# Modulation sums along weight rows on DVE, the first shift vector on TensorE, and layer 0's first input tiles completed pair by pair

## The reference

```python
c_act = jax.nn.silu(c)                                   # c is (1, 1024)
for l in range(2):
    mod = (c_act @ ada_w[l] + ada_b[l])[:, None, :]      # ada_w[l] is (1024, 6 * 1024) f32
    sh_m, sc_m, g_m, sh_f, sc_f, g_f = jnp.split(mod, 6, axis=-1)
    h = rms_norm(x, norm_mix_pre[l]) * (1 + sc_m) + sh_m
    x = x + g_m * rms_norm(hybrid_mixer(h, ...), norm_mix_post[l])
    h = rms_norm(x, norm_ffn_pre[l]) * (1 + sc_f) + sh_f
    x = x + g_f * rms_norm(ffn(h), norm_ffn_post[l])
```

## Time and profile before

| | |
|---|---|
| three runs | 1609.78, 1613.15, 1611.60 us; median 1611.6 us |
| profiled execution | 1613.58 us, of it the span of instructions 1611.8 us |
| busy share of the span | PE 95%, PEld 82%, DVE 84%, ACT 62%, POOL 4% |
| mean granted TensorE clock | 0.983 of full |
| DMA | 507.48 MB, mean 315 GB/s |
| PE busy and DMA share in slices of 40 us, first five | PE 3, 9, 9, 9, 9 tenths; DMA 9, 9, 5, 7, 6 tenths |

### The profile page before, as it was taken

One profiled execution on the slowest core, in us unless ns is written; L12 is line 12 of the kernel. 1 busy time (PEld: TensorE's weight loads), 2 busy tenths in 40 slices (PEclk: granted clock), 3 DMA queues, 4 the chain that ended last, 5 costly groups with the idle time before them and its releaser, 6 DMA issues.

```text
span 1611.8 us, 21543 instructions
## 1 busy us (share of the span) xinstructions
PE 1537.8 (95%) x8256; PEld 1328.5 (82%) x8256; DVE 1352.7 (84%) x1245; ACT 1007.1 (62%) x861; POOL 70.7 (4%) x99
## 2 busy tenths in 40 slices
PE   3999989999899998999999999999999999999995
PEld 3899979999789977888888887888887888888884
DVE  6987787775778867899899898899898899998885
ACT  3573443433456344777777777777777777777773
POOL 6000000000000000000000000000000000000000
PEclk9999999999999998999999999999999999999998
DMA  9957657775574862999999999999999999999990
GB/s 375 365 182 259 244 229 288 287 254 191 180 251 173 303 221 105 360 384 358 404 374 358 395 381 361 375 380 366 395 375 352 384 376 368 392 376 365 410 368 28
DMA packets 72705, 507.48 MB, mean 315 GB/s; under 512 B 8096, under 2 KB 8224, under 8 KB 13856
## 3 DMA queue, kind: packets, MB, share of 16 engines
q1 hardware_dynamic: 68528, 491.40, 79.8%
q0 software_dynamic: 4080, 14.69, 3.1%
HBM read 499.24 MB, written 6.82 MB: 314 GB/s over the span
## 4 chain that ended last, share of the span: by engine, by line
PE 89%; DVE 6%; ACT 2%; issue 1%; POOL 1%; DMA 0%; DVEq 0%; ACTq 0%; POOLq 0%
PE ps L1348 28%; PE ps L1350 27%; PE ps L1349 27%; PE ps L1744 1%; DVE lo L849 1%; DVE r L901 1%; PE ps L1387 1%; DVE lo L880 1%; DVE ada_acc L813 1%; PE ps L1511 1%; PE ps L1494 1%; PE ps L1367 1%; DVE x_tok L936 1%; DMA router_bias<-in_router_bias_dram 0%; ACT hi L515 0%
## 5 line engine op out<-in xcount | busy, mean ns | idle before, releaser
L880 DVE TENSOR_TENSOR lo<-raw,hi 128x2048 fp32r<-128x2048 f32 x336 | 764.8, 2290 | 96.9 <-ACT hi L515 96.4
L515 ACT ACTIVATE hi<-raw 128x2048 fp32r<-128x2048 f32 x336 | 644.8, 1919 | 200.4 <-PE ps L1350 200.4
L1348 PE MATMUL ps<-hi,hT_hi 128*128 128x512 f32 (+2 forms) x1088 | 428.9, 394 | 11.8 <-DVE hT_lo L907 4.8
L1350 PE MATMUL ps<-hi,hT_lo 128*128 128x512 f32 (+2 forms) x1088 | 420.8, 387 | 0.0
L1349 PE MATMUL ps<-lo,hT_hi 128*128 128x512 f32 (+2 forms) x1088 | 420.2, 386 | 0.0
L1348 PEld LDWEIGHTS ps<-hi,hT_hi 128*128 128x128 f32 x1088 | 205.2, 189 | 56.5 <-issue 8.4
L849 DVE TENSOR_TENSOR lo<-raw,hi 128x2048 fp32r<-128x2048 f32 (+2 forms) x87 | 190.1, 2190 | 62.0 <-ACT hi L499 60.6
L1350 PEld LDWEIGHTS ps<-hi,hT_lo 128*128 128x128 f32 x1088 | 205.1, 188 | 41.1
L1349 PEld LDWEIGHTS ps<-lo,hT_hi 128*128 128x128 f32 x1088 | 205.5, 189 | 38.2 <-issue 0.5
L1348 PE MATMUL ps<-hi,bT_hi 128*128 128x512 f32 (+1 forms) x576 | 226.7, 394 | 1.8 <-DVE bT_lo L1259 1.8
L499 ACT ACTIVATE hi<-raw 128x2048 fp32r<-128x2048 f32 (+2 forms) x87 | 158.3, 1824 | 108.5 <-PE ps L1350 105.4
(11 more groups left out here) (259 smaller groups left out, 1227.5 us busy)
## 6 DMA issues: line engine op xcount, KB each, us to landing
raw<-in_moe_w_dram SPq DMA_DIRECT2D x336, 1024.0 KB, 7.1
raw<-in_w_ada_dram SPq DMA_DIRECT2D x48, 1024.0 KB, 5.2
raw<-in_w_fg_dram SPq DMA_DIRECT2D x11, 1024.0 KB, 5.3
raw<-in_w_fu_dram SPq DMA_DIRECT2D x11, 1024.0 KB, 5.1
raw<-in_w_fd_dram SPq DMA_DIRECT2D x11, 1024.0 KB, 5.7
raw<-in_w_ga_dram SPq DMA_DIRECT2D x8, 1024.0 KB, 6.8
raw<-in_w_gb_dram SPq DMA_DIRECT2D x8, 1024.0 KB, 5.5
raw<-in_w_ab_dram SPq DMA_DIRECT2D x8, 1024.0 KB, 4.9
```

The costliest lines, as they stand in the source:

```text
L515: act.activation(hi[:, s, :], raw[:, slot, :], ACT.Copy).then_inc(hi_done, 1)
L880: dve.tensor_tensor(lo[:, s, :], raw[:, slot, :], hi[:, s, :].bitcast(f32), ALU.subtract).then_inc(raw_done, 1)
L1348: pe.matmul(o, wh, mh, start=first, stop=False)
L1350: return pe.matmul(o, wl, mh, start=False, stop=last)
```

## The change

Four things are changed together.

1. **Modulation weights by output channel.** The weights are laid out so that a partition holds one output channel's 1024 weights; a quarter holds two such blocks of 128 channels. `silu(c)` is repeated on all partitions (`cbc`, a broadcast DMA of 0.5 MB and one ACT pass), and DVE multiplies and sums along the row in one instruction (`scalar_tensor_tensor` with `accum_out`), which gives one finished column of the vector `av`. The sums over partitions on PE, and their uses on DVE, go away for shift and scale vectors. Gates build their diagonal in one DVE pass (`ada_gate`) and keep their two matmuls.
2. **The first shift vector on PE.** Its weights keep input channels on partitions (`w_ada0`); `shift_sum` makes 16 matmuls with one moving column per quarter, straight from `raw`; DVE adds the bias (`ada_shift`).
3. **The start pair by pair.** The stream brings shift and scale quarters alternately, x after the first of them, and the two cq chunks between them. Each quarter pair completes two channel blocks of scale and shift, and DVE, ACT and PE take up the layer input block pair by block pair. ACT's sine of the rotary angles moves behind the cq chunks.
4. **Layer 0's feed-forward shift vector** moves from chunks 2 to 5 to chunks 8 to 11 in `ADA_AT`.

```diff
-ADA_AT = [(0, SH_F, M0 + 2), (0, SC_F, M0 + 13), (0, G_M, M0 + 18),
+ADA_AT = [(0, SH_F, M0 + 8), (0, SC_F, M0 + 13), (0, G_M, M0 + 18),
...
-    out = [("ada", a, q) for a in range(len(ADA_FIRST)) for q in range(4)]
-    for s in range(NW):
+    out = []
+    for q in range(4):
+        if q >= 2:
+            out.append(("w", q - 2, 0))
+        out += [("ada", 0, q), ("ada", 1, q)]
+    for s in range(FIRST_W, NW):
...
+            sp.dma_start(cbc[:, :], A["c"].to_broadcast([P, D])).then_inc(cbc_in, 16)
...
-                if r == NRAW - 2:
+                if r == 0:
                     sp.dma_start(x[:, :, :], A["x"].rearrange("b (t p) d -> p (b t) d", p=P)).then_inc(x_in, 16)
...
+            act.wait_ge(cbc_in, 16)
+            act.activation(cbc[:, :], cbc[:, :], ACT.Silu).then_inc(cact_ready, 1)
...
             def mixer(l):
                 if l == 0:
-                    upto("m0.cq0", 1)
-                h_hi(2 * l)
+                    upto("m0.cq0", 0)
+                    h_hi(0, (0, 1))
+                    upto("m0.cq1", 0)
+                    h_hi(0, (2, 3))
...
-                if q == 0 and a > 1:
-                    dve.wait_ge(ada_full, sum(2 if ADA[b][1] in (G_M, G_F) else 1 for b in range(a)))
                 for kk in range(2):
                     w = raw[:, r % NRAW, kk * D:(kk + 1) * D]
-                    c = cact[:, 2 * q + kk:2 * q + kk + 1]
-                    if q == 0 and kk == 0:
-                        link(dve.tensor_scalar(ac[:, :], w, c, None, ALU.mult))
-                    else:
-                        m = dve.scalar_tensor_tensor(ac[:, :], w, c, ac[:, :], ALU.mult, ALU.add)
-                        if kk == 0:
-                            link(m)
+                    k = 2 * q + kk
+                    m = dve.scalar_tensor_tensor(w, w, 1.0, cbc[:, :], ALU.mult, ALU.mult, accum_out=av[:, k:k + 1])
                 m.then_inc(raw_done, 1)
                 dve.wait_ge(raw_done, r + 1)
-                if q == 3 and v in (G_M, G_F):
-
-                    for k in range(K):
-                        m = dve.scalar_tensor_tensor(ac[:, k * P:(k + 1) * P], ident[:, :], col(COL_ADA + (l * 6 + v) * K + k),
-                                                     ac[:, k * P:(k + 1) * P], ALU.mult, ALU.add)
...
+            def ada_scale(l, v, at, size):
+                n = 2 * l + (v >= SH_F)
+                what = AB[:, n, 0, at:at + size]
+                link(dve.tensor_tensor(what, av[:, at:at + size], ada_bias(l, v)[:, at:at + size], ALU.add))
...
+            def ada_gate(l, v):
+                link(dve.tensor_tensor(gv[:, :], av[:, :], ada_bias(l, v), ALU.add))
...
+                dve.tensor_tensor(gdiag.rearrange("p (k s) -> p k s", k=K), ident[:, :].unsqueeze(1).to_broadcast([P, K, P]),
+                                  gv[:, :].unsqueeze(2).to_broadcast([P, K, P]), ALU.mult).then_inc(gdiag_ready, 1)
+
+            def ada_shift(q):
+
+                r = RAW_OF["ada", 0, q]
+                dve.wait_ge(sh_full, q + 1)
+                dve.tensor_tensor(AB[:, 0, 1, 2 * q:2 * q + 2], ps[:, 7 - q % 2, 2 * q:2 * q + 2], ada_bias(0, SH_M)[:, 2 * q:2 * q + 2],
+                                  ALU.add).then_inc(raw_done, 1)
...
-            for q in range(4):
-                ada_quarter(0, q)
-            for q in range(4):
-                ada_quarter(1, q)
-                if q == 1:
-                    ada_use(0, 0)
-                    dve.wait_ge(pool_setup, 6)
...
+            ada_shift(1)
+            ada_quarter(1, 1)
+            h_full(0, 0)
+            h_full(0, 1)
             upto("m0.cq0", 0)
-            ada_use(1, 0)
+            h_rest(0, 0)
+            h_rest(0, 1)
+            ada_shift(2)
+            ada_quarter(1, 2)
+            h_full(0, 2)
+            upto("m0.cq1", 0)
+            h_rest(0, 2)
+            ada_shift(3)
+            ada_quarter(1, 3)
+            h_full(0, 3)
+            h_rest(0, 3)
...
-                else:
-                    for k in range(K):
-                        m = pe.matmul(ps[:, 7, k:k + 1], (r5 if a == 1 else acc)[:, k * P:(k + 1) * P], ones[:, 0:1], start=True, stop=True)
...
+            def shift_sum(q):
+
+                r = RAW_OF["ada", 0, q]
+                pe.wait_ge(raw_full[r % NRAW], 16 * (r // NRAW + 1))
+                if q >= 2:
+                    pe.wait_ge(raw_done, RAW_OF["ada", 0, q - 2] + 1)
+                for kk in range(2):
+                    for i in range(K):
+                        m = pe.matmul(ps[:, 7 - q % 2, 2 * q + kk:2 * q + kk + 1], raw[:, r % NRAW, i * 2 * P + kk * P:i * 2 * P + (kk + 1) * P],
+                                      cact[:, i:i + 1], start=(i == 0), stop=(i == K - 1))
+                m.then_inc(sh_full, 1)
...
             pe.wait_ge(pool_setup, 6)
-            ada_sum(0, 0)
+            pe.wait_ge(cact_ready, 1)
+            shift_sum(0)
+            shift_sum(1)
```

More of the change, by code:

```diff
@@ L135, in ada_sums @@
     out = []
[L136 to L142, removed]
-            else:
-                out.append((a, half, at + LAG_SUM * (1 + half), at + LAG_USE + LAG_SUM * half))
+    for a, (_, v, at) in enumerate(ADA_AT, len(ADA_FIRST)):
+        if v in (G_M, G_F):
+            gap = 2 if at in (M0 + 18, M1 + 18) else LAG_SUM
+            for half in range(2):
+                out.append((a, half, at + LAG_SUM + gap * half, at + LAG_USE + gap * half))
     return out
@@ L546, in y_norm, with h_hi @@
                     root(1, t)
-            def h_hi(n):
-                for b in range(4):
+            def h_hi(n, parts=range(4)):
+                for b in parts:
                     act.wait_ge(hf_ready, 4 * n + b + 1)
@@ new lines, in ada_bias @@
+            def ada_bias(l, v):
+                at = COL_ADA + (l * 6 + v) * K
+                return cols[:, at:at + K]
+            def ada_scale(l, v, at, size):
+                n = 2 * l + (v >= SH_F)
+                what = AB[:, n, 0, at:at + size]
+                link(dve.tensor_tensor(what, av[:, at:at + size], ada_bias(l, v)[:, at:at + size], ALU.add))
+                norm = COL_NORM + n * K + at
+                link(dve.scalar_tensor_tensor(what, what, 1.0, cols[:, norm:norm + size], ALU.add, ALU.mult))
@@ L830, in ada_use @@
                 dve.wait_ge(ada_full, sums[0])
-                n = 2 * l + (v >= SH_F)
-                if v in (G_M, G_F):
-                    gate, arrived = (gate_m, post_m_in) if v == G_M else (gate_f, post_f_in)
-                    dve.wait_ge(arrived, 16 * (l + 1))
-                    g = gate[:, half * 512:(half + 1) * 512]
-                    dve.tensor_tensor(g, ps[:, 7, :], g, ALU.mult).then_inc(ada_used, 1)
-                    dve.wait_ge(ada_used, sums[0])
-                    return
-                bias = cols[:, COL_ADA + (l * 6 + v) * K:COL_ADA + (l * 6 + v + 1) * K]
-                what = AB[:, n, 0 if v in (SC_M, SC_F) else 1, :]
-                dve.tensor_tensor(what, ps[:, 7, 0:K], bias, ALU.add).then_inc(ada_used, 1)
+                gate, arrived = (gate_m, post_m_in) if v == G_M else (gate_f, post_f_in)
+                dve.wait_ge(arrived, 16 * (l + 1))
+                g = gate[:, half * 512:(half + 1) * 512]
+                dve.tensor_tensor(g, ps[:, 7, :], g, ALU.mult).then_inc(ada_used, 1)
                 dve.wait_ge(ada_used, sums[0])
-                if v in (SC_M, SC_F):
-                    link(dve.scalar_tensor_tensor(what, what, 1.0, cols[:, COL_NORM + n * K:COL_NORM + (n + 1) * K], ALU.add, ALU.mult))
             def lo_part(s):
@@ L1379, in finish @@
                     if after == CHUNK[name]:
-                        ada_sum(a, half)
+                        ada_sum(half)
             def h_turn(n):
@@ L1404, in by_token @@
                     finish(f"m{l}.{name}{h}", m)
+                    if name == "cq" and l == 0 and h == 0:
+                        shift_sum(3)
             pe.wait_ge(pool_setup, 6)
-            ada_sum(0, 0)
+            pe.wait_ge(cact_ready, 1)
+            shift_sum(0)
+            shift_sum(1)
             def mixer(l):
@@ L1411, in mixer @@
                 if l == 0:
-                    ada_sum(1, 0)
+                    shift_sum(2)
                 by_token("cq", l, QR, (4, 5))
```

117 lines of the change are left out of this document (64 added, 53 removed).

## The result

| | before | after |
|---|---|---|
| median of the runs, us | 1612.34 (4 runs, 1609.78 to 1613.15) | 1628.29 (4 runs, 1624.1 to 1631.12) |
| profiled execution, us (span) | 1613.58 (1611.8) | 1627.61 (1625.9) |
| mean granted clock | 0.983 | 0.983 |

The ratio is 1.010, interval 1.0074 to 1.0125: 1.0% slower, and above the range given. I forecast +1.7 us and the profiled execution is 14.0 us longer.

A forecast was written before the change was run, and what follows sets the result against it. PE was taken to bound the kernel (89% of the span). Start +5.2, moved vector +4.5, five sums -8.4 and 0.4 for a clock dip make +1.7: 1611.6 to 1613.3 us, range 1606 to 1618.5.

The forecast's parts named there:

- The experts' part is untouched: Experts: the change was taken to leave their 336 chunks and slots as they were, so no term was given.
- Row passes: DVE's modulation quarters: a pass of 1024 elements takes 1.15 us, a quarter 2.43 instead of 2.63; worth nothing in all.
- The fourth case: DVE's row passes: half rate with the accumulator, 2.2 us for 1024 elements, +20 us, 1633 us; chance 0.04.
- Five sums, -8.4: Layer 0's mixer, dense part, layer 1's mixer: five sums over partitions leave full PE, 1.68 us each, -8.4 us.
- The start, +5.2: Start of layer 0: v begins at 61.1 us against 55.88 before, +5.2 us, bounds -3 and +9.
- The moved vector, +4.5: Layer 0's attention stretch: four quarters moved onto busy DVE delay the end of the scores by 4.5 us, bounds +2 to +8.
- The 0.4 us for a dip of the clock from 97 to 104 us: Layer 0's attention stretch: 0.4 us added for the chance that the clock dips in PE's waits.
- One-column sums keep the clock up: Start: rival, the first sum on PE brings the clock up, start -0.4, total -4.3, 1607.3 us; chance 0.27.
- DVE bounds the attention stretch: Layer 0, uq1 to last copy of k: rival, the stretch costs 8.6 us, 1617.0 us in all; chance 0.12.

The follow-up runs named there:

- e5: As e1, with layer 0's feed-forward shift vector (SH_F) back at its old place: 1604.18 us, ratio to before 0.9955.
- e8: As e1, with the first shift vector summed along rows on DVE and its four sums on PE gone: 1611.35 us, ratio to before 0.9986.
- e9: As e8, with layer 0's SH_F at its old place and the start in the order of the kernel before: 1600.75 us, ratio 0.9914.
- e1: The changed kernel with its two small tiles (av, gv) allocated behind everything else: 1611.01 us, ratio to before 0.9991.
- e2: The kernel before with only an unused tile of 64 bytes ahead of hT_hi: 1629.56 us, ratio 1.0107.
- e12: The kernel before with unused 64-byte tiles ahead of hi and of bT_hi, so only bT lies 64 bytes further from hi, lo: 1620.66 us, ratio 1.0054.
- e3: The changed kernel with an unused tile of 64 bytes more ahead of hT_hi, 128 in all: 1630.23 us, ratio to before 1.0107.
- e6: The kernel before with an unused tile of 64 bytes ahead of everything, distances between operands kept: 1615.53 us, ratio 1.0023.

## Why the prediction was wrong, point by point

**The step that failed** is the sentence "The experts' part is untouched: the same 336 chunks, the same slots." Its instructions are the same, but two small tiles moved half of their operands by 64 bytes, and that is worth +15 to +18 us: from the third transposition to the end, the nine traces with distance 0 (e5, e8 and e9 among them) give 1001.1 to 1007.2 us (mean 1004.1), the four with 32, 64 or 128 give 1020.7 to 1023.3 (mean 1022.0). Most of the scatter is the clock: multiplied by its mean granted clock (0.983 to 0.989) the stretch is 989.1 to 991.5 us in the nine and 1008.7 to 1010.0 in the four, 18.8 us apart. The 14.8 us between the first two traces are the low end. Shown by e1 (taken away in the changed kernel), e2 (added alone to the kernel before) and e12 (both distances in one program). I read the diff for instructions and order only. No rival had it either, and so the range could not reach it. The Trainium skill (TensorE: Matmul & The Clock Gate, "Step-by-step: what each phase is for") says that PE has two independent read ports for the operands, so that loading the next weights takes nothing from the running matmul. The rows of e12 show that a matmul's spacing does depend, by 5 to 7 ns, on how far its two operands lie apart; by which path the chip makes it so no run here shows.

**The other terms held within their bounds.** e1, the change without the shift, is at 0.9991 of before, -1.4 us (-3.7 to +0.6); I had said +1.7, 3 us more and outside that interval.

- *Row passes*: 1.15 us start to start, as taken. The fourth case (half rate, 1633) and with it the rule of the Trainium skill (Vector Engine (DVE) Microarchitecture Reference, "Points that are easy to get wrong") is refuted by these rows: two sources from SBUF with an accumulator start 1.15 us apart, and before, without one, 1.30 (two in 2.60). The time came near its figure, 1628 and 1633, for another reason: a number that fits is no evidence for its mechanism.
- *Five sums, -8.4*: scores to first transposition 113.7 us in e1 against 115.7 before, dense part 205.74 against 209.36, layer 1's mixer 177.85 against 181.44. That is -2.0, -3.6 and -3.6 for one, two and two sums: -9.2, or 1.84 for one, a little more than its row of 1.68. The shorter passes on DVE and the gates' diagonals, which I had put at nothing, are in this number too and are not measured apart.
- *The start, +5.2*: this start runs in four traces (the changed kernel, e1, e3, e5) and v begins at 62.3, 63.8, 58.5 and 58.3; the mean is 60.7, +4.8, where 61.1 was said. That the mean comes so near is partly luck, as the four lie 5.4 us apart. Against the old order with every sum on DVE (e9, 56.9) this start, pair by pair and with the first shift vector on PE, costs 3.8 in the traces and 3.4 between the medians of e5 and e9, both of which scatter by 9 to 11 us. With every sum on DVE the order pair by pair alone (e8, 59.3) costs 2.4, in one trace of each. The steps stand too: sums of 7 us at the low clock, a hole of 4 us inside cq1. The later sums, 4.8 and 3.6, came at a mix of both levels, as assumed.
- *The moved vector, +4.5*: +4.2 in the changed kernel, and -5.6 when put back (e5), which with a sum of 1.68 less is nearly the same term (the whole was 6.2). The 0.4 us for a dip of the clock from 97 to 104 us did not come: the granted clock there is 1.00.
- *One-column sums keep the clock up* (1607.3): refuted for the first two sums, 6.96 and 6.99 us in a row with 0.45 between. *DVE bounds the attention stretch*: it does, by the waits at uq1 and the scores, but by what the forecast had and no more.

What stays open: how the chip reads a matmul's two operands so that the distance matters, whether residues other than 0, 32, 64 and 128 behave the same, and the 3 us of e6. Also why a multiple of 256 bytes is the better distance at 512 columns and the worse at 256: the matmuls of 256 columns have the roles exchanged, `hT` moves and `hi` stands, and no run has the one without the other. At 384 columns, with the roles as at 512, the spacing is 174.1 ns before and 173.8 to 176.1 in the four kernels with another distance (layer 1's uq), so the roles alone do not decide.

## What to carry to other kernels

Where a change allocates a tile ahead of the operands of the main loop, compute the operands' addresses before and after; put small tiles behind the large ones, and keep a matmul's two operands at a distance that is a multiple of 256 bytes if it has 512 columns. When PE is full in both traces but does fewer instructions in the same window, look at the distance of starts, not at durations. And measure a bundle's parts apart: here the row sums in the old order gain 11 us, while the new start (about 4) and the moved vector (5 to 7) give nearly all of it back, and the placement alone costs 15 and more.

## What the runs showed of the hardware that I had not expected

- f32r matmuls back to back, 128 stationary columns: 512 moving columns start 227.5 ns apart where the distance of the two operands in a partition is a multiple of 256 bytes (also + 256, 512, 1024, or both moved by 64), and 233 ns at a residue of 32, 64 or 128. With 256 moving columns, and the two tiles in each other's role, it is the reverse, 120.0 against 116.7 to 118.7 ns.
- Between two executions of the same start the clock fell differently. From 30 to 37.5 us, in e1 and in e5, which have the same instructions up to there:

```profile
30.00:37.50 7.50, 7.50 (x47) 7.50 (x46) 6.16 (x12) 2.32 (x3) 0.00 (x0) 0.72 0.94 342
```

```profile
30.00:37.50 7.50, 7.50 (x56) 7.50 (x56) 7.36 (x14) 2.40 (x4) 0.00 (x0) 1.00 1.01 419
```

A granted clock of 0.72 (a mix of the 1.2 and 2.4 GHz levels) against 1.00: 47 matmuls against 56 in the same time, and v 5.4 us later in the one. One trace of such a start says less than its digits.
